# Modulation vector computed by VectorE with fused multiply-adds instead of by TensorE, twelve columns with two units each

## The chip, the cores and the metric

The kernel runs on one core of one Trainium2 chip. The metric is the device time of one execution in microseconds (us). Three runs before the change took 3199.53, 3201.83 and 3201.86 us; the median is 3201.83 us.

## The reference

The reference is one layer of a first block (a SwiGLU feed-forward, an attention and a state-space branch, a second SwiGLU feed-forward, an embedding gate, each with a layer norm) followed by one layer of a second block, all in float32. The change concerns two places of it:

```python
x = layer_norm(ALPHA * x + 0.5 * swiglu(x, ffn1_w1, ffn1_w3, ffn1_w2), ln1_g, ln1_b)   # first feed-forward
...
mod   = silu(c)     @ mod_w + mod_b     # second block: shift, scale, gate of the tokens
mod_k = silu(c_ctx) @ mod_w + mod_b     # and of the context
```

x has 1024 tokens by 1024 features; mod_w is 1024 by 3072, and c and c_ctx are one vector of 1024 numbers each. The modulation (the two vectors of 3072 numbers) depends on nothing else, and is first used by the context in the middle of the kernel. Both kernels compute it beside the first feed-forward.

## The kernel before

**Layout and engines.** Activations lie transposed, features on the 128 partitions and tokens along the free axis. Every float32 weight block is split by ScalarE into a rounded high part (type fp32r) and by VectorE into the rest, the low part, and a product takes three fp32r matmuls a block (high by high, high by low, low by high). Each engine's program is written out in a fixed order; engines wait for each other through semaphores, and each works strictly in its order.

**The columns of the feed-forward.** The hidden layer has 22 columns of 128 features, n = 0 to 21. From column 2 on a Strassen-like scheme computes the two up-projections of a column by seven products, m1 to m7, of 12 matmuls of 512 tokens each. Four weight sums (s1 to s4, done by `sums`, in four VectorE instructions) feed m5, m6, m7 and m3. VectorE adds the products up (`u2`, `c11`, `u3`, two in `c22`, `c21`, `c12`), ScalarE and VectorE make the hidden rows of both halves of the tokens (`mul`, then a high and a low part, `m_low` being the low one). The order is written out by `product_steps` (lines 31 to 52): for a column m2, m6, m5, m7, then, in even columns up to 18, a "down" step, then the modulation units of the column, then m1 of the next column, m4 and m3. The down step g adds the hidden columns 2g and 2g+1 into X: 16 groups of 6 matmuls, each read out of PSUM by one VectorE instruction. Down 0 stands inside column 2.

**Weights in flight.** A weight tile of 128 by 1024 float32 (512 KB) is loaded by SyncE into one of four raw slots (RAW has three, RAWX is the fourth). SyncE issues the loads in one fixed order and waits before each for the last reader of what lay in the slot (line 3564). Which slot a tile gets is settled by `lay_out` (line 145): the one whose present tile is read for the last time earliest in the order. The tile u1[n] (first up-projection, column n) serves m1 and m2 and, summed with u3[n], m5, m6, m7 and m3; u3[n] serves m4 too. The split halves lie in a ring of six places of 512 columns. In every step each engine calls `release` for the unit that it has finished, and `release` calls `halves`, which takes the next units in order, as far as their place and their raw slot are free in the order of the program, and splits them. So the split of a unit stands in the program about six units ahead of its product. `halves` of VectorE also does the sums of a column, one unit ahead of m6's own split (`sum_at`, line 379), and they wait until u3[n] has landed (line 2217).

**The modulation before.** A unit is a tile of mod_w, 256 input features by 512 outputs, 24 units in all (six output blocks m of four units). Each is split like any weight, and TensorE multiplies it by the split vectors silu(c), silu(c_ctx) (CVS, 4 columns) in 4 matmuls of 512 columns into PSUM bank 7, which is kept for it (the ring of banks has 7 others). After four units ScalarE copies the [4, 512] result to HELD, TensorE turns it in four small transposes (`mod_turn`), and VectorE adds up high and low and the bias into MOD. Columns 3, 5, 7 and 9 have two units, the others one.

Of the kernel before, what the change touches and what calls it, by code (L numbers as in the profile page):

```python
# [33 lines left out]
def product_steps(with_mod):  # L34


    out, mods = [], 0
    for n in range(2, 22):
        if 2 < n < 21:
            out.append(("m2", n))  # L40
        out.append(("m6", n))
        if n == 2:
            out.append(("down", 0))
        out += [("m5", n), ("m7", n)]
        if 2 < n < 19 and n % 2 == 0:
# [103 lines left out]
def lay_out(entries):  # L149
# [3 lines left out]
    for u, (kind, zone, loads, piece) in enumerate(entries):  # L153
        f = Form(kind, loads, piece)
        forms.append(f)
        if kind == "raw":
            continue
        if zone == "first" and base is None:
            base = [order[(at + i) % 5] for i in range(5)]
            ring, turn = [2 * k + i for k in base[:3] for i in range(2)], 0  # L160
        if zone == "ring":
            k = order[at % 5]
            at += 1
            f.places = (2 * k, 2 * k + 1)
# [41 lines left out]
    for u, f in enumerate(forms):  # L206
        f.raws = [ends[earlier[n]] for n in f.loads if n in earlier and forms[ends[earlier[n]]].kind == "raw"]
# [3 lines left out]
class Units:  # L211
# [10 lines left out]
    def next_half(self):  # L222

        while self.halved < self.limit:
            f = self.forms[self.halved]
            if not all(u in self.left for u in f.before + f.raws):
                return None
            self.halved += 1
            if f.kind not in ("raw", "hold"):
                return self.halved - 1  # L230
# [16 lines left out]
def build(nc, t, plan):  # L247
# [42 lines left out]
    CVS = at("CVS", 206, [128, 8, 4], F32R)  # L290
# [70 lines left out]
    CHI, CLO = CVS[:, :, 0:2], CVS[:, :, 2:4]  # L361
# [24 lines left out]
    banks, tmps, misc = Ring(7), Ring(NTMP), Ring(2)  # L386
# [144 lines left out]
    def tensor(e):  # L531
# [83 lines left out]
        def mod_turn(m):  # L615
            use = ("mt", m)
            banks.take(use, (ve, "mt", m))
            e.wait_ge(ac("mod", m), dma("const")("cols"), *banks.free(use))
            trs([(bank(*use)[:, 4 * j:4 * j + 4], HELD[0:4, m % 2, 128 * j:128 * j + 128], ident[0:4, 0:4])
                 for j in range(4)]).then_inc(*mm.inc(*use))  # L620

        def mod_unit(n):
            m, q = divmod(n, 4)
            if q == 0 and m:
                mod_turn(m - 1)
                e.wait_ge(ac("mod", m - 1))
            us = [w.take(), w.take()]
            e.wait_ge(w_hi(us[1]), w_lo(us[1]), ac("cvs"), ve("cvs"))
            mms([(PS[0:4, 7, :], CVS[:, 2 * q + k, :], blk(us[k], 0, 512)[r], q + k + r == 0, q + k + r == 5)
                 for k in range(2) for r in range(2)]).then_inc(*mm.inc("mod", n))  # L630
            for u in us:
                release(u)

        def ffn(name, tag, with_mod):
# [68 lines left out]
            for what, n in steps:  # L703
# [4 lines left out]
                elif what == "mod":  # L708
                    mod_unit(n)
# [7 lines left out]
            for m in range(4):  # L717
                down_open(m, last_parts(m))
                if m == 1 and with_mod:
                    mod_turn(5)  # L720
# [568 lines left out]
        banks.resize(8)  # L1289
        banks.ends[7] = ((ac, "mod", 5),)  # L1290
# [19 lines left out]
    def scalar(e):  # L1310
# [68 lines left out]
        def ffn(name, with_mod):  # L1379
# [38 lines left out]
            def mod_unit(n):  # L1418
                m, q = divmod(n, 4)
                us = [w.take(), w.take()]  # L1420
                if q == 3:
                    e.wait_ge(mm("mod", n))
                    if m > 1:
                        e.wait_ge(mm("mt", m - 2))
                    act(HELD[0:4, m % 2, :], PS[0:4, 7, :], ACT.Copy).then_inc(*ac.inc("mod", m))
                release(*us)

# [20 lines left out]
            for what, n in product_steps(with_mod):  # L1448
                if what == "mod":
                    mod_unit(n)  # L1450
                    continue
# [715 lines left out]
        act(CHI, cvec, ACT.Copy).then_inc(*ac.inc("cvs"))  # L2167
# [14 lines left out]
    def vector(e):  # L2182
# [112 lines left out]

        def mod_turn(m):
            e.wait_ge(mm("mt", m), dma("const")("cols"))
            part = bank("mt", m)[:, 0:16].rearrange("p (a r v) -> p a r v", a=4, r=2)
            out = MOD[:, 4 * m:4 * m + 4, :]
            tt(out, part[:, :, 0], col("mod_b", 4 * m, 4).unsqueeze(2).to_broadcast([128, 4, 2]), ALU.add).then_inc(*ve.inc("mt0", m))  # L2300
            e.wait_ge(ve("mt0", m))
            tt(out, out, part[:, :, 1], ALU.add).then_inc(*ve.inc("mt", m))

        def ffn(name, tag, with_mod, held):
# [99 lines left out]
            def mod_unit(n):  # L2404
                m, q = divmod(n, 4)
                if q == 0 and m:
                    mod_turn(m - 1)
                release(w.take(), w.take())

# [35 lines left out]
            for what, n in product_steps(with_mod):  # L2445
# [3 lines left out]
                if what == "mod":  # L2449
                    mod_unit(n)  # L2450
                    continue
# [43 lines left out]
            for m in range(8):  # L2495
                down_one(LAST, m, 0)
                if m == 1 and with_mod:
                    mod_turn(5)
# [1027 lines left out]
        e.wait_ge(ac("cvs"))  # L3526
        low(CLO, cvec, CHI).then_inc(*ve.inc("cvs"))
# [3 lines left out]
        ffn("ln1", "x", True, lambda h: mm("mt", 4 + h))  # L3531
# [23 lines left out]
    def sync(e):  # L3555
# [224 lines left out]
    for count in range(2):  # L3780
# [6 lines left out]
        banks.n = 7  # L3787
# [43 lines left out]
def ffn_units(w1, w3, w2, mod):  # L3831
# [17 lines left out]
    for what, n in product_steps(bool(mod)):  # L3849
# [15 lines left out]
        else:  # L3865
            if what == "down" and n == 0:
                forms.append(("hold", "hold", (), 0))
            for a in (down(columns_of(n)) if what == "down" else [mod[n]]):
# [148 lines left out]
```

## Time and profile before

| | us |
|---|---|
| median of three runs | 3201.83 |
| the profiled execution | 3202.06 |
| its span, first to last instruction | 3200.3 |
| TensorE busy (14840 matmuls) | 3126.6, 98% of the span |
| VectorE busy (4144 instructions) | 2400.2, 75% |
| ScalarE busy (1933 instructions) | 1240.3, 39% |

The profiled execution took 0.23 us more than the median of the runs, so its durations can be added to either. The chain that ended last is 88% TensorE, 7% VectorE and 4% ScalarE. Busy time of TensorE counts pipelined matmuls until their modelled end, so the distance from one start to the next, not the duration, says what a matmul costs in a stream.

### The profile page before, as it was taken

The numbers are of one execution on the slowest core, as the hardware profiler recorded it, in microseconds if no ns is written. First come the engines' busy times: TensorE is split into PE (matmuls) and PEld (weight loads), VectorE is DVE, ScalarE is ACT, GpSimd is POOL, SyncE is SP. The second block draws the span as 40 slices with busy tenths as digits, with TensorE's granted clock in tenths as the row PEclk, the third lists the DMA queues.
The fourth block names the chain that finished last, engine by engine and source line by source line (L and its number), as shares of the span: only waits on it lengthen the run. The fifth ranks groups of instructions, "written<-read, shape, count | busy, mean of one in ns | idle before, by whom it ended". The sixth has DMA issues, their size and how long they took to land.

```text
span 3200.3 us, 37931 instructions
## 1 busy us (share of the span) xinstructions
PE 3126.6 (98%) x14840; PEld 2543.1 (79%) x14840; DVE 2400.2 (75%) x4144; ACT 1240.3 (39%) x1933; POOL 2.2 (0%) x9
## 2 busy tenths in 40 slices
PE   8999999999999999988999999999999999999998
PEld 7887888877988877777887888888777688788887
DVE  6777777778869588878588766667788789789736
ACT  4333233335242456655243223223355533423414
POOL 0000000000000000000000000000000000000000
PEclk9999999999999999999999999999999999999999
DMA  3222211213433450002311111111211321122242
GB/s 128 73 79 77 68 66 66 73 60 126 130 82 130 142 190 8 7 27 74 151 53 47 60 46 53 60 47 53 66 53 53 112 70 70 40 77 97 78 168 73
DMA packets 89249, 250.68 MB, mean 78 GB/s; under 512 B 8560, under 2 KB 24304, under 8 KB 87536
## 3 DMA queue, kind: packets, MB, share of 16 engines
q1 hardware_dynamic: 89072, 248.25, 22.4%
q8 instruction: 119, 1.95, 0.2%
q14 instruction: 58, 0.48, 0.0%
HBM read 204.18 MB, written 44.04 MB: 78 GB/s over the span
## 4 chain that ended last, share of the span: by engine, by line
PE 88%; DVE 7%; ACT 4%; issue 1%; DMA 0%; DVEq 0%; SPq 0%; ACTq 0%
PE PS L543 86%; PE PS L548 2%; DVE WS L2187 1%; DVE X L2195 1%; DVE XS L2195 1%; DVE X L2187 1%; ACT PT L1314 1%; ACT TMP L1792 1%; DVE HELD L2244 1%; DVE COLB L2995 1%; ACT XS L1314 0%; DVE XSf L2187 0%; DVE TMP L2187 0%; DVE PT L2187 0%; ACT WS L1314 0%
## 5 line engine op out<-in xcount | busy, mean ns | idle before, releaser
L543 PE MATMUL PS<-XS,WS 128*128 128x512 f32 (+1 forms) x6480 | 1515.7, 391 | 18.8 <-DVE XS L2187 8.7
L543 PEld LDWEIGHTS PS<-XS,WS 128*128 128x128 f32 x6480 | 1208.8, 188 | 294.5 <-issue 28.2
L543 PE MATMUL PS<-HS,WS 128*128 128x512 f32 x2208 | 512.5, 391 | 3.1 <-DVE TMP L2187 2.7
L543 PEld LDWEIGHTS PS<-HS,WS 128*128 128x128 f32 x2208 | 415.2, 188 | 93.6 <-DVE TMP L2187 3.5
L2187 DVE TENSOR_TENSOR WS<-RAW,WS 128x512 fp32r<-128x512 f32 (+1 forms) x403 | 353.4, 885 | 178.5 <-ACT WS L1314 177.9
L1314 ACT ACTIVATE WS<-RAW 128x512 fp32r<-128x512 f32 (+1 forms) x403 | 312.8, 782 | 404.6 <-PE PS L543 350.2
L2187 DVE TENSOR_TENSOR X<-PS,X 128x512 f32<-128x512 f32 x272 | 184.3, 689 | 101.7 <-PE PS L543 101.6
L2187 DVE TENSOR_TENSOR TMP<-TMP,PS 128x512 f32<-128x512 f32 x304 | 203.8, 683 | 65.5 <-PE PS L543 59.3
L543 PE MATMUL PS<-T,WS 128*128 128x512 f32 x960 | 230.6, 389 | 0.0
L543 PEld LDWEIGHTS PS<-T,WS 128*128 128x128 f32 x960 | 180.2, 188 | 37.4
L1314 ACT ACTIVATE TMP<-PS 128x512 f32<-128x512 f32 x144 | 85.0, 595 | 303.2 <-PE PS L543 299.6
L2195 DVE SCALAR_TENSOR_TENSOR CV<-UU,COL,CV 128x1024 f32<-128x1024 f32 x120 | 154.1, 1284 | 3.4
L1314 ACT ACTIVATE HS<-TMP 128x512 fp32r<-128x512 f32 x88 | 55.6, 632 | 210.4 <-DVE TMP L2195 196.3
L543 PE MATMUL PS<-KH,QH 128*128 128x512 f32 x384 | 109.0, 422 | 2.3 <-DVE QH L2187 2.3
L543 PE MATMUL PS<-T1h_ln,WS 128*128 128x512 f32 x320 | 105.0, 389 | 0.0
L2187 DVE TENSOR_TENSOR PT<-PS,PT 128x512 fp32r<-128x512 f32 x128 | 82.2, 683 | 15.5 <-ACT PT L1314 15.2
L1314 ACT ACTIVATE PT<-PS 128x512 fp32r<-128x512 f32 x128 | 69.8, 595 | 56.8 <-PE PS L548 55.6
L1314 ACT ACTIVATE TMP<-TMP 128x512 f32<-128x512 f32 x80 | 50.6, 632 | 101.4 <-DVE TMP L2187 101.4
L2187 DVE TENSOR_TENSOR HS<-TMP,HS 128x512 fp32r<-128x512 f32 x88 | 60.7, 689 | 32.3 <-ACT HS L1314 32.1
L1314 ACT ACT_TABLE_LOAD x56 | 71.8, 1283 | 32.8 <-DVE GG L2187 27.1
L543 PEld LDWEIGHTS PS<-KH,QH 128*128 128x128 f32 x384 | 70.4, 196 | 14.5 <-ACT VH L1314 2.5
L543 PE MATMUL PS<-MH,WS 128*128 128x512 f32 x256 | 80.4, 393 | 0.0
(334 smaller groups left out, 3628.7 us busy)
## 6 DMA issues: line engine op xcount, KB each, us to landing
RAW<-in_W SPq DMA_DIRECT2D x263, 512.0 KB, 3.3
RAWX<-in_W SPq DMA_DIRECT2D x30, 512.0 KB, 3.2
DC<-TMP SPq DMA_DIRECT2D x32, 256.0 KB, 2.0
X<-in_xT SPq DMA_DIRECT2D x8, 512.0 KB, 9.3
DX<-X SPq DMA_DIRECT2D x2, 2048.0 KB, 9.0
DCZ<-CA SPq DMA_DIRECT2D x8, 512.0 KB, 4.3
DGA<-TMP SPq DMA_DIRECT2D x16, 256.0 KB, 2.2
DGB<-TMP SPq DMA_DIRECT2D x16, 256.0 KB, 3.3
```

Source lines behind the costliest of these rows:

```text
L543: done = d.matmul(out, l, r, start=first, stop=last)
L548: done = d.transpose(out, x, idn)
L1314: return d.activation(out, x, f, bias=bias, scale=scale)
L1792: d.activation(PROB[n % 3], PS[:, 2 + 2 * (n % 2):4 + 2 * (n % 2), :], ACT.Exp, bias=nb, scale=SCALE, accum_out=sm).then_inc(*ac.inc("ex", n))
L2187: return d.tensor_tensor(out, a, b, op)
L2195: return d.scalar_tensor_tensor(out=out, in0=a, scalar=s, in1=b, op0=op0, op1=op1)
L2244: d.reciprocal(out[:, 0:width], tmp("rs", name, h)[:, 0:width]).then_inc(*ve.inc("rs", name, h))
L2995: d.tensor_reduce(mx, PS[:, 2 + 2 * (n % 2):4 + 2 * (n % 2), :], AX.XY, ALU.max).then_inc(*ve.inc("mx", n))
```

## The change

The 24 units keep their tiles and their order, but are no longer split. For each unit VectorE runs four instructions on [128, 512]: for each of its two row blocks and each of the two vectors it multiplies the raw tile by the vector's column of 128 numbers (a scalar per partition) and adds to HELD. After four units TensorE sums HELD over the partitions: 8 float32 matmuls (4 blocks of 128 outputs by 2 vectors) with HELD as the weights and one column of ones as the moving operand, which leaves the outputs on the partitions; VectorE adds the bias. In the order two units stand in columns 2, 3, 5, 6, 8, 9, 11, 12, 14, 15, 17 and 18, and a turn at the end of columns 4, 7, 10, 13, 16 and 19. The units get a kind of their own, "vec": no place in the ring of six, and a raw slot that is free once VectorE's fourth instruction is done. The sums of a column move from the unit before m6 to m6 itself, in both feed-forwards. Bank 7 joins the ring of PSUM banks (8 instead of 7).

```diff
@@ product_steps
-        if with_mod:
-            for _ in range(2 if n in (3, 5, 7, 9) else 1):
-                out.append(("mod", mods))
-                mods += 1
+        if with_mod and n < 20 and n % 3 != 1:
+            out += [("mod", mods), ("mod", mods + 1)]
+            mods += 2
         out += [("m1", n + 1) if n < 21 else ("m2", n), ("m4", n), ("m3", n)]
+        if with_mod and n % 3 == 1 and n < 20:
+            out.append(("turn", mods // 4 - 1))
@@ lay_out
-        if kind == "raw":
+        if kind in ("raw", "vec"):
             continue
...
-        f.raws = [... forms[ends[earlier[n]]].kind == "raw"]
+        f.raws = [... forms[ends[earlier[n]]].kind in ("raw", "vec")]
@@ build
-            sum_at[u if pieces[0] == u - 2 else min(u, pieces[1])] = f.loads
+            sum_at[u] = f.loads
-    banks, tmps, misc = Ring(7), Ring(NTMP), Ring(2)
+    banks, tmps, misc = Ring(8), Ring(NTMP), Ring(2)
@@ tensor
         def mod_turn(m):
             use = ("mt", m)
             banks.take(use, (ve, "mt", m))
-            e.wait_ge(ac("mod", m), dma("const")("cols"), *banks.free(use))
-            trs([(bank(*use)[:, 4 * j:4 * j + 4], HELD[0:4, m % 2, 128 * j:128 * j + 128], ident[0:4, 0:4])
-                 for j in range(4)]).then_inc(*mm.inc(*use))
-        def mod_unit(n):
-            ... (waits for both halves, 4 matmuls into PS[0:4, 7, :])
+            e.wait_ge(ve("mv", 4 * m + 3), ve("ones"), *banks.free(use))
+            for j in range(4):
+                for v in range(2):
+                    done = d.matmul(bank(*use)[:, 2 * j + v:2 * j + v + 1], HELD[:, v, 128 * j:128 * j + 128], ones[:, 0:1],
+                                    start=True, stop=True)
+            done.then_inc(*mm.inc(*use))
@@ scalar
-        def mod_unit(n):
-            ... (copies PS[0:4, 7, :] to HELD after every fourth unit)
@@ vector
+        def mod_unit(n):
+            m, q = divmod(n, 4)
+            u = w.take()
+            e.wait_ge(*loaded(u), ac("cv"))
+            for k in range(2):
+                for v in range(2):
+                    x, c = HELD[:, v, :], cvec[:, 2 * q + k, v:v + 1]
+                    if q + k == 0:
+                        d.tensor_scalar(x, raw(u, 512 * k, 512), c, None, ALU.mult).then_inc(*ve.inc("ms", n, k, v))
+                    else:
+                        e.wait_ge(ve("ms", n, 0, v) if k else ve("ms", n - 1, 1, v))
+                        stt(x, raw(u, 512 * k, 512), c, x, ALU.mult, ALU.add).then_inc(*ve.inc("ms", n, k, v))
+            ve.same("mv", n)
+            ve.same("vec", u)
+            release(u)
@@ sync, loads
-                    e.wait_ge(mm("unit", u) if forms[u].kind == "raw" else w_lo(u))
+                    e.wait_ge(mm("unit", u) if forms[u].kind == "raw" else ve("vec", u) if forms[u].kind == "vec" else w_lo(u))
@@ ffn_units
+            if what == "mod":
+                forms.append(("vec", "turning", (load(mod[n]),), 0))
```

The rest of the diff takes out what the old way needed: the tile CVS and its two instructions, the turn of the last block after the products, and the steps that kept bank 7.

## Rows read from the trace of the kernel before

**Rows 1.** The page, busy time, share and instructions of each engine.

```profile
PE 3126.6 (98%) x14840; PEld 2543.1 (79%) x14840; DVE 2400.2 (75%) x4144; ACT 1240.3 (39%) x1933; POOL 2.2 (0%) x9
```

**Rows 2.** Busy time in the stretch of the columns; TensorE, loads, VectorE, ScalarE, POOL, clock, DMA.

```profile
90.00:655.00 565.00, 564.32 (x2498) 456.11 (x2497) 402.96 (x635) 184.81 (x312) 0.00 (x0) 1.00 0.21 72
```

**Rows 3.** The chain of waits, 60 to 700 us: start, length, what (one piece).

```profile
240.92 0.59 ACT HELD L1314
```

**Rows 4.** TensorE in order of time: start, duration, what.

```profile
114.02 2.02 PE L543 MATMUL PS<-WS,CVS 128*4 128x512 f32 x8
115.88 2.92 PE L543 MATMUL PS<-XS,WS 128*128 128x512 f32 x12
...
176.79 0.41 PE L548 MATMUL PS<-ident,HELD 4*128 4x4 f32 x4
177.12 2.01 PE L543 MATMUL PS<-WS,CVS 128*4 128x512 f32 x8
...
366.74 1.09 PE L543 MATMUL PS<-WS,CVS 128*4 128x512 f32 x4
367.67 2.92 PE L543 MATMUL PS<-XS,WS 128*128 128x512 f32 x12
370.42 2.88 PE L543 MATMUL PS<-T,WS 128*128 128x512 f32 x12
```

**Rows 5.** Weight loads in order of time: start, duration, what.

```profile
1015.47 1.98 PEld L543 LDWEIGHTS PS<-KM,UB 128*128 128x128 f32 x16
1017.36 1.68 PEld L543 LDWEIGHTS PS<-XS,WS 128*128 128x128 f32 x8
```

**Rows 6.** Groups of weight loads by shape: busy, mean ns, idle before.

```profile
L543 PEld LDWEIGHTS PS<-HELD,ones 128*128 128x128 f32 x26 | 4.5, 188 | 7.9 <-DVE HELD L2187 6.8 <-issue 0.5
L543 PEld LDWEIGHTS PS<-WS,CVS 128*4 128x4 f32 x96 | 7.7, 85 | 10.9 <-issue 0.3
```

**Rows 7.** VectorE in order of time: start, duration, what, idle before.

```profile
366.94 0.69 DVE L2187 TENSOR_TENSOR TMP<-TMP,PS 128x512 f32<-128x512 f32 x1 [1.36 <-PE PS L543]
367.54 0.68 DVE L2187 TENSOR_TENSOR RAW<-RAW,RAWX 128x512 f32<-128x512 f32 x1
...
370.07 0.69 DVE L2187 TENSOR_TENSOR WS<-RAW,WS 128x512 fp32r<-128x512 f32 x1
...
374.46 0.69 DVE L2195 SCALAR_TENSOR_TENSOR TMP<-TMP 128x512 f32<-128x512 f32 x1
376.37 0.69 DVE L2187 TENSOR_TENSOR WS<-RAW,WS 128x512 fp32r<-128x512 f32 x1 [1.22 <-ACT WS L1314]
...
379.49 0.68 DVE L2195 SCALAR_TENSOR_TENSOR TMP<-TMP 128x512 f32<-128x512 f32 x1
380.88 0.69 DVE L2187 TENSOR_TENSOR HS<-TMP,HS 128x512 fp32r<-128x512 f32 x1 [0.70 <-ACT HS L1314]
...
707.46 0.74 DVE L2195 SCALAR_TENSOR_TENSOR XS<-X,COL,XS 128x512 fp32r<-128x512 f32 x1
708.12 0.74 DVE L2195 SCALAR_TENSOR_TENSOR X<-X,COL,HELD 128x512 f32<-128x512 f32 x1
```

**Rows 8.** A VectorE group by shape: busy, mean ns, idle before.

```profile
L2191 DVE TENSOR_SCALAR TMP<-ident,COLB 128x128 f32<-128x128 f32 x64 | 18.4, 287 | 2.3
```

**Rows 9.** DMA issues, 300 to 500 us: KB each, us from issue to landing.

```profile
RAW<-in_W SPq DMA_DIRECT2D x20, 512.0 KB, 3.3
```

**Rows 10.** Half a microsecond each behind the issue at 399.21 us; last columns DMA share, GB/s.

```profile
400.20:400.70 0.50, 0.50 (x4) 0.42 (x3) 0.16 (x1) 0.00 (x0) 0.00 (x0) 1.00 0.92 311
...
401.20:401.70 0.50, 0.50 (x3) 0.39 (x3) 0.03 (x1) 0.00 (x0) 0.00 (x0) 1.00 0.82 328
```

**Rows 11.** Two microseconds each around TensorE's idle stretch; the clock is third from the end.

```profile
64.00:66.00 2.00, 0.48 (x3) 0.05 (x1) 1.97 (x4) 0.51 (x1) 0.00 (x0) 1.00 0.74 258
66.00:68.00 2.00, 1.51 (x5) 1.25 (x6) 2.00 (x4) 0.33 (x1) 0.00 (x0) 0.84 0.75 227
68.00:70.00 2.00, 2.00 (x6) 1.55 (x5) 2.00 (x5) 2.00 (x4) 0.00 (x0) 0.50 0.84 236
70.00:72.00 2.00, 2.00 (x8) 1.60 (x8) 2.00 (x5) 2.00 (x5) 0.00 (x0) 0.80 0.16 66
```

More of the change, by code:

```diff
@@ L206, in lay_out @@
     for u, f in enumerate(forms):
-        f.raws = [ends[earlier[n]] for n in f.loads if n in earlier and forms[ends[earlier[n]]].kind == "raw"]
+        f.raws = [ends[earlier[n]] for n in f.loads if n in earlier and forms[ends[earlier[n]]].kind in ("raw", "vec")]
     return forms, slots, earlier, ends
@@ L228, in next_half @@
             self.halved += 1
-            if f.kind not in ("raw", "hold"):
+            if f.kind not in ("raw", "vec", "hold"):
                 return self.halved - 1
@@ L289, in build @@
     HELD = at("HELD", 202, [128, 2, 512], F32)
-    CVS = at("CVS", 206, [128, 8, 4], F32R)
     HS = at("HS", 152, [128, NHS, 2, 1024], F32R)
@@ L360, in build @@
     ACf = at("ACf", 152, [128, 2, 4, 1024], F32)
-    CHI, CLO = CVS[:, :, 0:2], CVS[:, :, 2:4]
     cvec, STAT, GL = COLB[:, 0:16].rearrange("p (k v) -> p k v", v=2), COLB[:, 32:64], COLB[:, 64:96]
@@ L617, in mod_turn @@
             banks.take(use, (ve, "mt", m))
-            e.wait_ge(ac("mod", m), dma("const")("cols"), *banks.free(use))
-            trs([(bank(*use)[:, 4 * j:4 * j + 4], HELD[0:4, m % 2, 128 * j:128 * j + 128], ident[0:4, 0:4])
-                 for j in range(4)]).then_inc(*mm.inc(*use))
-        def mod_unit(n):
[L623 to L632, printed above, removed]
+            e.wait_ge(ve("mv", 4 * m + 3), ve("ones"), *banks.free(use))
[4 more added lines that the diff above has]
+            done.then_inc(*mm.inc(*use))
         def ffn(name, tag, with_mod):
@@ L708, in ffn @@
                 elif what == "mod":
-                    mod_unit(n)
+                    release(w.take())
+                elif what == "turn":
+                    mod_turn(n)
                 else:
@@ L718, in ffn @@
                 down_open(m, last_parts(m))
-                if m == 1 and with_mod:
-                    mod_turn(5)
             for m in range(8):
@@ L1288, in tensor @@
         ffn("ln1", "x", True)
-        banks.resize(8)
-        banks.ends[7] = ((ac, "mod", 5),)
         latents()
@@ L1416, in turned @@
                     act(hi(k), lo(k), ACT.Copy).then_inc(*ac.inc(name, what, k))
-            def mod_unit(n):
[L1419 to L1426, printed above, removed]
             us = {fi: (w.take(), w.take()) for fi in (0, 1)}
@@ L1448, in ffn @@
             for what, n in product_steps(with_mod):
+                if what == "turn":
+                    continue
                 if what == "mod":
-                    mod_unit(n)
+                    release(w.take())
                     continue
@@ L2166, in scalar @@
         e.wait_ge(ac("cv"))
-        act(CHI, cvec, ACT.Copy).then_inc(*ac.inc("cvs"))
         ffn("ln1", True)
@@ L2294, in norm @@
                     yield
+        def mod_unit(n):
[13 more added lines that the diff above has]
+            release(u)
         def mod_turn(m):
             e.wait_ge(mm("mt", m), dma("const")("cols"))
-            part = bank("mt", m)[:, 0:16].rearrange("p (a r v) -> p a r v", a=4, r=2)
             out = MOD[:, 4 * m:4 * m + 4, :]
-            tt(out, part[:, :, 0], col("mod_b", 4 * m, 4).unsqueeze(2).to_broadcast([128, 4, 2]), ALU.add).then_inc(*ve.inc("mt0", m))
-            e.wait_ge(ve("mt0", m))
-            tt(out, out, part[:, :, 1], ALU.add).then_inc(*ve.inc("mt", m))
+            tt(out, bank("mt", m)[:, 0:8].rearrange("p (a v) -> p a v", v=2),
+               col("mod_b", 4 * m, 4).unsqueeze(2).to_broadcast([128, 4, 2]), ALU.add).then_inc(*ve.inc("mt", m))
         def ffn(name, tag, with_mod, held):
@@ L2402, in turned @@
                 low(lo, f, hi).then_inc(*ve.inc(name, what, k))
[L2404 to L2408, printed above, removed]
             def down_one(g, m, h):
@@ L2450, in ffn @@
                     mod_unit(n)
+                    continue
+                if what == "turn":
+                    mod_turn(n)
                     continue
@@ L2496, in ffn @@
                 down_one(LAST, m, 0)
-                if m == 1 and with_mod:
-                    mod_turn(5)
                 norm_add(name, m, 0, X, x_now, held(0))
@@ L3525, in vector @@
         halves()
-        e.wait_ge(ac("cvs"))
-        low(CLO, cvec, CHI).then_inc(*ve.inc("cvs"))
         e.wait_ge(dma("const")("cols"))
@@ L3530, in vector @@
         tt(DB, col("ln2_b", 4, 4), col("ln2_b", 0, 4), ALU.subtract).then_inc(*ve.inc("db"))
-        ffn("ln1", "x", True, lambda h: mm("mt", 4 + h))
+        ffn("ln1", "x", True, lambda h: mm("mt", 5))
         latents()
@@ L3786, in build @@
             ring.restart()
-        banks.n = 7
+        banks.n = 8
     for s in signals.values():
@@ L3867, in ffn_units @@
                 forms.append(("hold", "hold", (), 0))
-            for a in (down(columns_of(n)) if what == "down" else [mod[n]]):
+            for a in down(columns_of(n)) if what == "down" else ():
                 k = load(a)
                 forms += [("cols", "turning", (k,), 0), ("cols", "turning", (k,), 1)]
+            if what == "mod":
+                forms.append(("vec", "turning", (load(mod[n]),), 0))
     for j, a in enumerate(down(columns_of(LAST))):
```

## The prediction

> **What bounds the kernel now.** I read the page first: TensorE is busy 98% of the span, VectorE 75% [rows 1]. Then the stretch of the changed columns, 90 to 655 us: TensorE idles 0.7 us in 565, VectorE works 403 us, 71% [rows 2]. So a matmul taken out shortens the kernel by its whole spacing, and one put in lengthens it; VectorE's work is free as long as its results come before TensorE asks for them. Next TensorE in order of time, for spacings: a product of 12 matmuls takes 2.72 to 2.75 us from start to start (367.67 to 370.42) [rows 4], 0.227 us a matmul, so a down group of 6 takes 1.36. Last VectorE in order of time and the loads, because the change makes both late.
>
> **TensorE's part.** Removed: a single unit holds 0.93 us (366.74 to 367.67), a pair 1.86 (114.02 to 115.88), a turn of four transposes 0.33 (176.79 to 177.12) [rows 4]. 16 singles 14.9, 4 pairs 7.4, 6 turns 2.0; ScalarE's copy to HELD stood in the chain once, 0.6 [rows 3]. Sum 24.9 us. Added: 48 float32 matmuls. The trace counts a float32 matmul twice (the layer norms' sums of ones by HELD have two records each, 26 for 13 [rows 6]), so a turn is 16 weight loads with 16 matmuls of one column. The nearest rows are 16 loads of the same shape in 1.89 us (1015.47 to 1017.36), 0.118 each, beside matmuls of 128 columns [rows 5]. I take 2.1 us a turn with its start, 12.5 in all. Bounds: the spacing of the old turn's transposes, 0.083 us [rows 4], 8 us in all; the whole length of a load, 0.188 [rows 6], 18 us. Net on TensorE: 12.4 us less.
> A load of 128 columns is 103 ns longer than one of 4, 0.83 ns a column [rows 6]. The Trainium skill (TensorE: Matmul & The Clock Gate, LDWEIGHTS) gives the columns over 1.2 GHz, by itself 107 ns for 128; the turns would be 10.2 us by it instead of 12.5.
>
> **VectorE's part.** Removed: 48 low halves at 0.60 us from start to start. Added: 96 instructions with a column of scalars; the like ones run 0.66 apart (707.46 to 708.12) [rows 7]. That is 63 less 29 us, 34 more: 437 of some 550 us, 80%. On average it fits. I price all 96 alike: the 12 with one tensor operand could be faster, but a TENSOR_SCALAR of 128 elements takes 287 ns [rows 8].
> By the Trainium skill (VectorE: DVE Perf Modes, Mode 2x_2P) a float32 operation with a single tensor source in SBUF makes two elements a cycle; those 12 would save VectorE 3 us, which changes the kernel by less than 1. The 84 with two tensors stay at one, which is what speaks against the change.
>
> **The new wait.** Before, a unit's raw slot came free with its split, about six units ahead of its use. Now it comes free only when VectorE has done the unit in its place. By the rule of the layout (the slot whose tile is read last earliest), in all twelve columns the first unit of the pair has the slot that u3[n+1] needs. So VectorE finishes the first unit and calls `release`; the next thing in its program is the sums of column n+1, which need u3[n+1], whose load SyncE issues only now. VectorE stands for the whole load, 3.3 us [rows 9]; its second unit, the splits and the product sums of the next steps are queued behind it, and ScalarE stands in its own program at the high part of that sum. From the landing, four sums take 2.53 us and the low half of m6 0.69 (367.54 to 370.07) [rows 7]. TensorE needs m6 of column n+1 four products, 10.9 us, after the modulation step. I write the time since TensorE began m1 (t = 0).
>
> *Odd column after an unloaded one (5, 11, 17).* VectorE takes up m7 at 0.2 (366.94 against 366.74), adds `u3` and both `c22`, starts the unit at 2.0, has it done at 4.7; load to 8.1; low half of m6 done at 11.3. TensorE waits 0.4. Then the other low half, the second unit, and the column's steps with the waits for ScalarE that rows show: 1.91 us from `mul` to the low half behind it, 1.39 from `mul` to the next `m_low` [rows 7]. The hidden rows of the column are done at 20.5 and 23.8. TensorE wants them for the down step at 19.5: it waits 1.0, runs one group, waits 1.9. In the down column itself u1[n+2] lies in the slot of the second down tile, whose last split is the unit just before it; VectorE stands for another load and its high half, the last `c22` ends at 33.5, and the seventh down group, which needs that PSUM bank among the eight, wants it at 30.6: 2.9. Together 6.2 us, three times: 18.6.
> *Even column (6, 8, 12, 14, 18).* The last group is read at once, the unit starts at 0.9, m6 is ready at 10.2, before 10.9. No wait there.
> *Odd column right after a loaded one (9, 15; 3 is like it).* VectorE is already late: second unit of column 8 done at 13.4, low half of m7 at 14.0. Only then are issued, in one order, the loads of two modulation tiles and of u1[n+1]. A transfer holds the DMA engines some 1.4 us (400.2 to 401.7) [rows 10], so the third lands at 19.6; its high and low half are ready at 21.0, TensorE wants m1 at 19.0: 2.0. The rest of the column takes VectorE 9.5 us (ten starts at 0.60 to 0.70 and two waits of 0.7 to 0.8), so the next first unit starts at 29.8, is done at 32.5, its load lands at 35.9, m6 is ready at 39.1, wanted at 31.9: 7.2. The hidden rows are ready at 48.3 and 51.6, wanted from 47.3: 1.0 and 1.9. Together 12.1 us; columns 9 and 15: 24.2. At columns 2 and 3, where m5 and m7 stand between down 0 and the first unit, the same working gives 13.3.
> *Columns 7 to 8 and 13 to 14*: the turn gives VectorE 2.1 us; 0.4 us remain each, 0.8.
> Waits in all: 57 us. Bounds: nothing, if VectorE's lead covers all of it; and 12 waits of 3.3, 8 later waits of 3.9 for u1 and the 34 us of work, all uncovered, 105.
>
> **The clock.** After an idle stretch of 2 us before 66.5 TensorE's clock was granted at 0.84, 0.50 and 0.80 in three stretches of 2 us: 1.7 us lost at the lower level, 1.2 GHz [rows 11]. The three waits of 7 us should bring it down each time. Most of the loss only uses up the wait that follows (VectorE, not TensorE, sets the next step); I add 4 us, bounds 0 and 20 (twelve waits of 1.7).
>
> **Hidden edits.** Taking 48 high halves from ScalarE, the sums one unit later and CVS are worth nothing: ScalarE works 185 us of 565 [rows 2] and the sums stand five products ahead; uncovered, the sums' move costs 0.6 us a column. The eighth bank is in the working above; with seven, the down waits would be 1.4 us longer.
>
> **Sum.** 3202.1 (the profiled execution, 0.2 above the median of the runs) - 12.4 + 57 + 4 = 3250.7; I say 3250.
>
> **Rivals.**
> A, faster: VectorE's lead hides everything. For it: 29% of VectorE is idle now [rows 2], a split has five products, 13.6 us, before its use, and a down step gives VectorE slack for 12 us. Against it: m6's split has four products and a load in it. Then only TensorE's net counts: 3202 - 12 = 3190. It decides if VectorE starts the first unit within some 1.5 us of TensorE's m1 and never falls more than 10.9 us behind in the odd columns.
> B, about even: the units cost their work, but the loads are not waited for, because the slots fall otherwise than I read them, or a load lands by the time VectorE comes to it. VectorE is then 5.3 us late per pair instead of 9 to 13; only the odd columns after loaded ones reach TensorE, three times 2 to 6 us and some clock: 3202 - 12 + 16 = 3206.
> C, slower still: VectorE sets the pace for most of the stretch, since each wait leaves the next step later than my chains carry over and the loads queue. VectorE's work 437, its waits for ScalarE now 60 or so, 12 loads of 3.3 and 8 of 3.9, and the part of its idle time in down steps that can't be used, some 50: 617 us for a stretch of 565 before, 3202 + 52; with the clock at 1.2 GHz after most waits, 20, and turns at 18 us, 3280 to 3290.
>
> **Chances.** Forecast 0.58, A 0.10, B 0.13, C 0.19. For the likeliest alone 3225 to 3275. The range leaves out A and half of C: 3203 to 3285. A change under 0.2% (6.4 us) can't be told from none. B lies on that line and is split between same and slower: faster 0.10, same 0.07, slower 0.83.
>
> **What would show it.** In the profile after: the 96 and 24 matmul records of the old way gone and 96 of the turns there, a turn near 2 us. VectorE waiting for the DMA of RAW, a dozen times near 3.3 us, right behind its fourth instruction on HELD. TensorE waiting for WS (m6, m1) and for HS (down) in the stretch from 90 us, some 57 us in all, the longest near 7 us in columns 3, 9 and 15, and clock below 1.00 behind them; the second feed-forward unchanged. If VectorE never waits for RAW, the slot step is wrong (B); if it does and TensorE doesn't wait, my count of the lead is wrong (A); if the gain on TensorE isn't near 12 us, the turns are.

## The result, and the profile after

The change made the kernel slower: 3241.02 us, the median of 4 runs (3239.27 to 3242.18), against 3201.28 in the same session (3199.53 to 3201.86). The ratio is 1.0123, 95% interval 1.0112 to 1.0135. The forecast was 3250 and slower. The execution profiled after has a span of 3240.4 us, 40.1 more than before.

The page of the changed kernel answers to [rows 1]: TensorE does 2 points less of a longer span, with nearly the same busy time. The second block is the stretch of the columns, answering to [rows 2] (busy of TensorE, weight loads, VectorE, ScalarE, POOL, then clock, DMA share, GB/s): 43 us of 605 without a matmul where it was 0.7 of 565, and a clock of 0.98.

```profile
PE 3123.4 (96%) x14816; PEld 2548.2 (79%) x14816; DVE 2419.9 (75%) x4185; ACT 1205.0 (37%) x1878; POOL 2.2 (0%) x9
```
```profile
90.00:695.00 605.00, 561.71 (x2471) 459.71 (x2470) 424.74 (x679) 151.26 (x260) 0.00 (x0) 0.98 0.19 68
```

Next the view of waits in 80 to 690 us: who waits for what, us in total, times, the longest. TensorE first.

```profile
PE PS L542 <- ACT WS L1302: 23.5, 5, 6.9
PE PS L542 <- DVE HS L2166: 9.5, 9, 1.7
PE PS L542 <- DVE TMP L2166: 7.6, 5, 2.4
PE PS L542 <- DVE WS L2166: 2.7, 1, 2.7
```

VectorE in the same stretch. Before, there was no wait of VectorE for a tile of weights here. Now there are twelve of 3.3 us. The releaser reads "issue" because the profile ties none to them; the times of the load below do.

```profile
DVE WS L2166 <- ACT WS L1302: 84.5, 49, 5.1
DVE RAW L2166 <- issue: 36.4, 11, 3.4
...
DVE RAWX L2166 <- issue: 3.4, 1, 3.4
```

One of them in order of time (start, duration, engine, what, count, idle before). The pair of column 8 begins at 295.80. Its first unit is done at 298.0; at 298.03 SyncE issues the next load of its queue (it issued none between 274.3 and then); the sums, which need that tile, start at 301.34. After the second unit (305.08, done at 307.8) VectorE stands again, now because ScalarE's high half of m1 is not made.

```profile
295.80 0.87 DVE L2283 TENSOR_SCALAR HELD<-RAW,COLB 128x512 f32<-128x512 f32 x2
296.59 1.41 DVE L2174 SCALAR_TENSOR_TENSOR HELD<-RAW,COLB,HELD 128x512 f32<-128x512 f32 x2
301.34 0.69 DVE L2166 TENSOR_TENSOR RAW<-RAW 128x512 f32<-128x512 f32 x1 [3.34 <-issue]
...
305.08 2.73 DVE L2174 SCALAR_TENSOR_TENSOR HELD<-RAWX,COLB,HELD 128x512 f32<-128x512 f32 x4
...
314.93 0.69 DVE L2166 TENSOR_TENSOR WS<-RAW,WS 128x512 fp32r<-128x512 f32 x1 [5.11 <-ACT WS L1302]
```

That second stop is the load of u1: SyncE's rows show three loads going out together when the second unit is done, and u1 is the last.

```profile
307.84 0.33 SPq L3553 DMA_DIRECT2D RAWX<-in_W  x1
308.21 0.91 SPq L3553 DMA_DIRECT2D RAW<-in_W  x2
```

TensorE in order of time, the first 350 us (the later columns repeat these waits within 0.2 us; the last row is cut off where the view ends). In turn: m1 and m6 of column 3, its hidden row; a turn and the two products behind it; the three waits of columns 5 and 6, two for hidden rows and one for a PSUM bank; a bank; m1, m6 and a hidden row of column 9.

```profile
113.11 2.98 PE L542 MATMUL PS<-XS,WS 128*128 128x512 f32 x12 [2.69 <-DVE WS L2166]
131.02 5.19 PE L542 MATMUL PS<-T,WS 128*128 128x512 f32 x12 [6.77 <-ACT WS L1302]
143.36 20.65 PE L542 MATMUL PS<-HS,WS 128*128 128x512 f32 x90 [0.33 <-DVE HS L2166]
172.01 1.84 PE L620 MATMUL PS<-ones,HELD 128*128 128x1 f32 x16
173.71 3.03 PE L542 MATMUL PS<-XS,WS 128*128 128x512 f32 x12
176.57 2.88 PE L542 MATMUL PS<-T,WS 128*128 128x512 f32 x12
204.65 1.61 PE L542 MATMUL PS<-HS,WS 128*128 128x512 f32 x6 [0.68 <-DVE HS L2166]
207.94 7.05 PE L542 MATMUL PS<-HS,WS 128*128 128x512 f32 x30 [1.68 <-DVE HS L2166]
217.29 15.49 PE L542 MATMUL PS<-HS,WS 128*128 128x512 f32 x60 [2.31 <-DVE TMP L2166]
281.22 13.94 PE L542 MATMUL PS<-HS,WS 128*128 128x512 f32 x60 [0.35 <-DVE TMP L2166]
315.72 3.01 PE L542 MATMUL PS<-XS,WS 128*128 128x512 f32 x12 [1.53 <-ACT WS L1302]
333.76 4.57 PE L542 MATMUL PS<-T,WS 128*128 128x512 f32 x12 [6.87 <-ACT WS L1302]
346.29 3.88 PE L542 MATMUL PS<-HS,WS 128*128 128x512 f32 x16 [1.15 <-DVE HS L2166]
```

Last the clock around the wait before 333.76, in windows of 2 us, answering to [rows 11]; it is the third figure from the end. TensorE works 0.24 us of the first window and all of the two others; the clock is 0.50, 0.50, then 0.71.

```profile
332.00:334.00 2.00, 0.24 (x1) 0.27 (x2) 2.00 (x4) 1.79 (x4) 0.00 (x0) 0.50 0.01 4
334.00:336.00 2.00, 2.00 (x5) 1.57 (x6) 2.00 (x4) 0.36 (x1) 0.00 (x0) 0.50 0.03 8
336.00:338.00 2.00, 2.00 (x8) 1.62 (x7) 2.00 (x4) 0.00 (x0) 0.00 (x0) 0.71 0.12 18
```

Below, "the clock's loss" of a run is worked out in one way for all: stretches of 4 us from 80 to 690 us, in each TensorE's busy time times what the granted clock lacks to 1.00, summed. It is 0.0 us before and 7.0 after.

### The profile page after: what moved, and what is told of

It is laid out like the page before. It is cut to its first block, busy times and chain, and to the rows that moved or that the text cites. A ratio compares the mean times of both kernels' runs of the same rounds, so it can differ in the third digit from the quotient of the medians.

```text
span 3240.4 us, 37839 instructions
## 1 busy us (share of the span) xinstructions
PE 3123.4 (96%) x14816; PEld 2548.2 (79%) x14816; DVE 2419.9 (75%) x4185; ACT 1205.0 (37%) x1878; POOL 2.2 (0%) x9
## 4 chain that ended last, share of the span: by engine, by line
PE 69%; DVE 7%; ACT 4%; issue 1%; DMA 0%; DVEq 0%; ACTq 0%; SPq 0%
PE PS L542 67%; PE PS L547 2%; DVE WS L2166 1%; DVE X L2174 1%; DVE XS L2174 1%; DVE X L2166 1%; ACT PT L1302 1%; DVE COLB L2983 1%; ACT TMP L1772 1%; DVE HELD L2223 1%; ACT XS L1302 0%; DVE TMP L2166 0%; DVE XSf L2166 0%; DVE PT L2166 0%; ACT WS L1302 0%
## 5 line engine op out<-in xcount | busy, mean ns | idle before, releaser
L2166 DVE TENSOR_TENSOR WS<-RAW,WS 128x512 fp32r<-128x512 f32 (+1 forms) x373 | 333.2, 900 | 208.1 <-ACT WS L1302 207.9
L1302 ACT ACTIVATE WS<-RAW 128x512 fp32r<-128x512 f32 (+1 forms) x373 | 292.9, 795 | 352.0 <-PE PS L542 270.6
L542 PE MATMUL PS<-T,WS 128*128 128x512 f32 x960 | 236.5, 396 | 20.6 <-ACT WS L1302 20.6
L2166 DVE TENSOR_TENSOR TMP<-TMP,PS 128x512 f32<-128x512 f32 x304 | 202.7, 682 | 54.2 <-PE PS L542 47.9
L542 PEld LDWEIGHTS PS<-T,WS 128*128 128x128 f32 x960 | 183.9, 192 | 60.6 <-ACT WS L1302 21.7
L1302 ACT ACTIVATE WS<-S2T 128x512 fp32r<-128x512 f32 x40 | 25.3, 633 | 278.8 <-DVE S2T L2166 256.8
```

Of the source, the lines that this page charges most:

```text
L542: done = d.matmul(out, l, r, start=first, stop=last)
L1302: return d.activation(out, x, f, bias=bias, scale=scale)
L2166: return d.tensor_tensor(out, a, b, op)
```

## The experiments

The theory of places: a unit's tile keeps its place until VectorE has worked on it, the next column's tiles must wait for that place, and their loads are what TensorE ends up waiting for. The rival, the theory of work: the 96 instructions, 60 us of VectorE (84 start 0.66 apart, 12 start 0.40 apart; the expectations below say 64) in place of 29 us of low halves, use up its lead whatever the loads do. Edits are made to the changed kernel unless another is named. The runs of the kernel before beside the first four had a median of 3201.6.

**One: the first unit is given up with the second.** Since VectorE takes splits in the order in which units are given up, it now does both units and then the sums.

```
-            release(u)
+            if n % 2:
+                release(u - 1, u)
```

> VectorE frees the raw slots and splits the next units only after the second unit of a pair; instructions, loads and their order are the same. Slot theory (VectorE stands for the load of u3[n+1] behind the first unit, and everything behind it comes late): the second unit's 2.65 us now lie under the load, so VectorE's twelve waits of 3.35 us shrink to about 0.7. All that comes behind the second unit is 2.65 us earlier: at columns 5/6, 11/12 and 17/18 TensorE's waits for the hidden rows (0.7 and 1.7 us) and for the PSUM bank (2.3) go to nothing; at 9, 15 and 3 the wait before m1 (1.5) goes, the one before m6 falls from 6.9 to about 4.2, the one for the hidden rows goes. Waits 43 to about 13 us, with some clock: 3205 us (3200 to 3212). Work theory (it is VectorE's 34 us more of work that TensorE waits for, the load wait only stands where VectorE would have been idle): the same work in the same place, 3230 us or more.

3209.49 us (3206.22 to 3212.28), ratio to before 1.0023 [1.0012, 1.0033]. The load goes out at 289.11, VectorE does its second unit meanwhile, and the sums wait 0.95 us instead of 3.34:

```profile
287.67 1.41 DVE L2174 SCALAR_TENSOR_TENSOR HELD<-RAW,COLB,HELD 128x512 f32<-128x512 f32 x2
288.99 2.73 DVE L2174 SCALAR_TENSOR_TENSOR HELD<-RAWX,COLB,HELD 128x512 f32<-128x512 f32 x4
292.68 0.69 DVE L2166 TENSOR_TENSOR RAW<-RAW 128x512 f32<-128x512 f32 x1 [0.95 <-issue]
```

The same instructions in another order give back 32 of the 40 us. Between the two profiled executions, 30.5 us apart, 25.1 lie before the end of the block; the other 5.4 lie behind it, where the programs are the same, and are not the edit's. TensorE's waits fall from 43.3 to 18.5 us, while the clock's loss is 9.8 in the execution that was profiled (3211.69 us, on the long side of this kernel's).

**Two: no tile, the same work.** The 24 loads and their places are gone; VectorE's 96 instructions read rows of X instead. The modulation is then of the wrong data.

```
-                forms.append(("vec", "turning", (load(mod[n]),), 0))
+                forms.append(("vec", "turning", (), 0))
...
-                        d.tensor_scalar(x, raw(u, 512 * k, 512), c, None, ALU.mult)
+                        d.tensor_scalar(x, X[:, 2 * q + k, 0:512], c, None, ALU.mult)
...
-                        stt(x, raw(u, 512 * k, 512), c, x, ALU.mult, ALU.add)
+                        stt(x, X[:, 2 * q + k, 0:512], c, x, ALU.mult, ALU.add)
```

> The 24 units have no tile and no raw slot; VectorE runs the same 96 instructions in the same places, on rows of X instead (the modulation is not what it should be: this leaves out the 24 loads). Slot theory: no wait for a load, u3 and u1 are in their slots early, TensorE's waits in the columns go to under 3 us; what is left is the gain of TensorE (14 us on the columns, 3 us on the first down step, 2 us given back behind the first feed-forward): 3187 us (3183 to 3193). Work theory: the work is unchanged, so at least half of the waits stay: 3215 us or more.

3184.11 us (3183.29 to 3186.41), ratio 0.9946 [0.9931, 0.9961]. TensorE waits 1.2 us in 60 to 700, the clock loses nothing. This is the theory of work tried alone, and it falls: all of that work fits beside TensorE. It also gives the change's worth without its places, 17.5 us faster, and the price of the places, 3241.0 - 3184.1 = 56.9 us.

**Three: half the work, all the places.** Only the first row block of each unit is added up, so half of the modulation's sum is left out.

```
-            for k in range(2):
+            for k in range(1):
...
-                        e.wait_ge(ve("ms", n, 0, v) if k else ve("ms", n - 1, 1, v))
+                        e.wait_ge(ve("ms", n - 1, 0, v))
```

> Each unit runs only the two instructions of its first row block (half of the modulation's sum is left out); tiles, slots, loads and the order stay. VectorE's work on the units is then 32 us, about the 29 of the low halves that it replaced. Slot theory: VectorE still waits 3.35 us for u3[n+1] in the twelve columns; the columns are earlier by 1.3 us a unit, which leaves waits of about 3 us before m6 at columns 4, 10 and 16 and little else, some 9 us with a little clock: 3197 us (3192 to 3204), not down to the 3187 of no load wait. Work theory: with no work added nothing is left of the waits: 3187 us. If the two effects only add up, without one needing the other, the waits fall by the share of the work removed, about 34 of 74 us: 3217.

3220.76 us (3219.24 to 3227.24), ratio 1.0058 [1.0041, 1.0074]: a miss, 24 us above what I expected from my own theory, and near the 3217 that I had written down for two effects that only add up. I had let the waits shrink by the work taken out. The trace (of the execution of 3227.24 us, 6.5 above the median) shows VectorE's waits whole: VectorE stands 44 us for tiles, more than the 39.8 of the full version (one of them 4.67 us), and TensorE's waits for m6 go only from 6.9 to 5.7.

```profile
DVE RAW L2166 <- issue: 40.1, 11, 4.7
DVE RAWX L2166 <- issue: 3.9, 1, 3.9
```

**Four: seven banks until the end of the block.** (The line that sets the ring to seven where the program starts anew is left out below.)

```
-    banks, tmps, misc = Ring(8), Ring(NTMP), Ring(2)
+    banks, tmps, misc = Ring(7), Ring(NTMP), Ring(2)
...
         ffn("ln1", "x", True)
+        banks.resize(8)
```

> Seven PSUM banks in the ring through the first feed-forward, as before the change, eight behind it; all else as after. If the eighth bank is what took 3 us off the first down step (its second group waited 2.0 us before and the clock fell behind it), this comes back; and the waits for a bank in the down steps of columns 6, 12 and 18 (2.3 us), 8 and 14 (0.3) each grow by the length of one group, 1.4. In all some 10 us more than the changed kernel: 3251 us (3246 to 3256). If the down step's gain is from elsewhere (the fewer splits of ScalarE): 3248 or less, with the first down step unchanged.

3261.73 us (3259.89 to 3267.28), ratio 1.0190 [1.0175, 1.0205]: 20.7 more than the change, twice what I expected and above my range. Its parts in the block, by the traces: 2.7 us in the first down step (below); TensorE's waits in 80 to 690 us 54.2 instead of 43.3, so 10.9, most of it in the bank waits (4.20 where eight banks have 2.31, 4.53 where they have 2.28); and the clock, which loses 14.0 instead of 7.0. Together 20.6. The two profiled spans are only 17.7 apart, since behind the block this one is 4.3 shorter. I had left the clock out. The first down step, seven banks and then eight (the kernel before has 2.01 us there too):

```profile
66.22 22.29 PE L542 MATMUL PS<-HS,WS 128*128 128x512 f32 x90 [2.01 <-DVE TMP L2167]
88.35 0.39 PE L542 MATMUL PS<-T1h_ln,WS 128*128 128x512 f32 x1
```
```profile
66.41 19.36 PE L542 MATMUL PS<-HS,WS 128*128 128x512 f32 x84 [0.63 <-DVE TMP L2166]
85.61 0.39 PE L542 MATMUL PS<-T1h_ln,WS 128*128 128x512 f32 x1
```

**Five: all the places, less work still.** To settle the third run's miss, the 84 multiply-adds are cut to 16 of 512 columns, so that most of the modulation's sum is left out. It does not take all the work away: 84 at 0.15 us and 12 multiplications at 0.40 are 17 us, where half the work was 29 and the whole is 60.

```
-                        stt(x, raw(u, 512 * k, 512), c, x, ALU.mult, ALU.add)
+                        x = x[:, 0:16]
+                        stt(x, raw(u, 512 * k, 16), c, x, ALU.mult, ALU.add)
```

> The changed kernel with its 24 loads, their places and their order, but the 84 multiply-adds of the units work on 16 of 512 columns (12 full multiplications stay), so that nearly all of VectorE's 64 us of added work is gone; the modulation's values are therefore not the reference's. Halving the work before left 3221. If time is a sum of a part for places and one that falls in step with the work: 3221 - (3241 - 3221) = 3201 (range 3197 to 3206). If the load's landing sets the waits and the work between hardly counts any more: 3208 to 3221.

3218.28 us (3216.45 to 3219.75), ratio 1.0049 [1.0034, 1.0064]. The additive guess falls, though by less than the expectation has it, which took all the work for gone: 31 us of work less gave 20.3 us in the third run, so 12 less would give 8 here, and 2.5 came. The other outcome, 3208 to 3221, holds. The pair of column 8 shows why so little is left to gain. The two units' instructions take 1.7 us instead of 4.8, and VectorE stands 4.13 us for u3 and then 5.06 for the high half of m1, whose tile was the last of three loads that went out from 294.40 to 295.35, and was read by ScalarE at 300.77:

```profile
285.46 0.38 DVE L2174 SCALAR_TENSOR_TENSOR HELD<-RAW,COLB,HELD 128x16 f32<-128x16 f32 x2
289.96 0.69 DVE L2166 TENSOR_TENSOR RAW<-RAW 128x512 f32<-128x512 f32 x1 [4.13 <-DMA RAW<-in_W]
...
293.70 0.67 DVE L2174 SCALAR_TENSOR_TENSOR HELD<-RAWX,COLB,HELD 128x16 f32<-128x16 f32 x4
...
301.44 0.69 DVE L2166 TENSOR_TENSOR WS<-RAW,WS 128x512 fp32r<-128x512 f32 x1 [5.06 <-ACT WS L1302]
```

So some 34 of the 56.9 us (3218.3 - 3184.1) stay with 17 of the 60 us of work. By the rows of this pair they are two landings in a row, with VectorE's and ScalarE's programs held behind them; with no work at all it wasn't tried. The other 23 go with 43 us of work, which costs only because the landings have used up the lead (the second run has the whole work at no cost).

**Six and seven: another placement.** One unit in every column, and a second one in four odd columns only. By the layout's rule the next column's two tiles should then take places of earlier splits, except behind the four pairs. In the seventh run the pairs are deferred as in the first.

```
+        turn = with_mod and mods // 4
-        if with_mod and n < 20 and n % 3 != 1:
-            out += [("mod", mods), ("mod", mods + 1)]
-            mods += 2
+        if with_mod:
+            for _ in range(2 if n in (3, 5, 9, 11) else 1):
+                out.append(("mod", mods))
+                mods += 1
...
-        if with_mod and n % 3 == 1 and n < 20:
+        if with_mod and mods // 4 > turn:
```

> One modulation unit in every column 2 to 21, a second one in columns 3, 5, 9 and 11 (always an odd column, and never the end of one group of four and the start of the next in one column); each sum over the partitions stays behind the last unit of its four. The work of VectorE and TensorE is that of the change to the instruction; what differs is that after a single unit the next column's two weight tiles no longer take a place that a unit of the same column must leave first. Theory of places (the waits are loads that find their place held by a unit): only the four pairs are left, each worth what a loaded odd column followed by an even one cost there, some 5 to 7 us with the clock, so 3184 + 4 x 6 = 3208, range 3196 to 3214. Theory of work (64 us more of VectorE in these columns use up its lead): no better than the change, 3235 to 3245.

3204.44 us (3202.11 to 3206.68), ratio 1.0008 [0.9999, 1.0018]. VectorE stands for a tile four times, 13.9 us in all, instead of twelve times and 39.8.

```
-            release(u)
+            if n not in (1, 4, 9, 12):
+                release(*((u - 1, u) if n in (2, 5, 10, 13) else (u,)))
```

> The placement of the kernel just named, and in the four columns with two units the first one is given up (for the order in which VectorE takes its splits) only together with the second, so that VectorE does both before it waits for the tile that goes to the first one's place. Theory of places: each pair costs 3 us less, 3196, range 3188 to 3204, and so faster than the kernel before or equal to it. If what is left in the kernel just named is not VectorE's wait for that tile, the two are equal within 3 us.

3192.43 us (3191.76 to 3193.47), ratio 0.9970 [0.9958, 0.9981]: faster than the kernel before. VectorE's work is that of the change; deferring four pairs is worth 12.0 us, the 3 each that were expected. Waits of TensorE in the seventh run, 80 to 690 us, all of them:

```profile
PE PS L544 <- DVE HS L2168: 3.2, 1, 3.2
PE PS L544 <- ACT WS L1304: 1.6, 3, 1.1
```

**Eight: done by column 19, as in the change.** Six deferred pairs (columns 3, 5, 9, 11, 15, 17), nothing in columns 20 and 21; edits to the seventh run's kernel.

```
-        if with_mod:
-            for _ in range(2 if n in (3, 5, 9, 11) else 1):
+        if with_mod and n < 20:
+            for _ in range(2 if n in (3, 5, 9, 11, 15, 17) else 1):
...
-            if n not in (1, 4, 9, 12):
-                release(*((u - 1, u) if n in (2, 5, 10, 13) else (u,)))
+            if n not in (1, 4, 9, 12, 17, 20):
+                release(*((u - 1, u) if n in (2, 5, 10, 13, 18, 21) else (u,)))
```

> Two units in columns 3, 5, 9, 11, 15 and 17, one in the other columns 2 to 19, none behind column 19; in each pair the first unit is given up with the second. Against the version with one unit in columns 20 and 21 too (3192.4) it takes away the one long wait left there, 3.2 us of TensorE in front of the last tiles, whose place was a unit's, and adds two pairs, each worth about 0.5 us by the pairs already there (1.6 us of waits for conversions on four). Theory of places: 3192.4 - 3.2 - a little clock + 1 = 3190, range 3186 to 3193. Were a pair dear in itself, 3195 or more.

3188.14 us (3186.9 to 3189.52), ratio 0.9957 [0.9945, 0.9970]. This is the version that beats both kernels: 14 us under the one before, 53 under the change, 4 above the version without tiles. It has all 24 loads and all the work, so neither the traffic of the loads nor the work is what cost 57 us. Its TensorE waits 2.3 us in 60 to 690, and its clock loses nothing.

**Nine: the banks behind the block.** In all versions with eight banks from the start TensorE waits 3.7 us at a place of the attention where it didn't before. The eighth run has:

```profile
1171.42 4.50 PE L544 MATMUL PS<-CKV,WS 128*128 128x512 f32 x12 [3.68 <-DVE TMP L2168]
1186.06 2.99 PE L544 MATMUL PS<-KH,QH 128*128 128x512 f32 x12 [0.30 <-DVE QH L2168]
1188.89 2.21 PE L544 MATMUL PS<-CQ,WS 128*128 128x512 f32 x9
```

The edit to the eighth run's kernel moves the ring on by five, so that later uses get their old banks.

```
         ffn("ln1", "x", True)
+        for _ in range(5):
+            banks.skip()
```

> The kernel just named, and behind the first feed-forward block the ring of eight PSUM banks is moved on by five places, so that the latents and the attention behind take the banks that they took before the change (316 uses modulo 7 is place 1; modulo 8 it is 4). In every version with eight banks from the start TensorE waits 3.7 us for one bank in the attention, and in none where the later stages kept the old banks. If that wait is the banks' phase: 3.5 us less than the kernel just named, range 2 to 5 less. If it is only put off (the stretch behind has other waits of VectorE that then grow), 0 to 1.5 us less: the changed kernel lost 2.1 us behind the block in all.

3194.59 us (3191.7 to 3196.58), ratio to before 0.9977 [0.9967, 0.9986]: 6.4 us slower than without it (4.7 between the profiled spans), a miss. The shift lands on the most recently used banks, which VectorE is still adding to X, and TensorE waits 6.86 us at once:

```profile
705.02 10.05 PE L544 MATMUL PS<-XS,WS 128*128 128x512 f32 x36 [6.86 <-DVE X L2170]
```

The wait of 3.68 us is gone, so it is indeed the banks' phase. But it was hardly worth anything: TensorE now waits 2.33 us for QH a little later (as it does in the kernel before) and has the 12 matmuls behind it in 4.57 instead of 2.99 us, and it waits 0.4 us at each of two places between. The ninth run is 5.03 us behind the eighth in front of this stretch (1139.76 against 1134.73, a row of matmuls on ZG) and 4.46 us at its end (1193.35 against 1188.89), so 0.6 us came back. The wait was put off, the other outcome that the expectation names.

```profile
1188.94 4.57 PE L544 MATMUL PS<-KH,QH 128*128 128x512 f32 x12 [2.33 <-DVE QH L2170]
1193.35 2.21 PE L544 MATMUL PS<-CQ,WS 128*128 128x512 f32 x9
```

A shift at a quieter place wasn't tried; by these rows it could win some 0.6 us.

## Why the prediction was right, and where its sizes were off

The sign, the mechanism and the place hold: a load is issued only when VectorE has done the first unit, twelve times, 3.3 us each as [rows 9] has it; the runs on order, places and work make it the cause (all 56.9 us go with the places, and 53 of them with another order of the same loads and instructions). By the steps:

- **TensorE's part**: forecast 12.4 us less, measured 13.9 less. That is the 24.9 removed, as read from the rows before, less the turns. A turn runs from 172.01 to 173.71, and the product behind it takes 2.86 us to the next start (176.57) instead of 2.72, so a turn costs 1.84; six are 11.0 against 12.5. The second run, whose TensorE waits for nothing in these columns, bears the sum out: it reaches the end of the block 17.4 us before the kernel before (700.77 against 718.16, the same row), of which 3.0 are the first down step. The weight loads of a turn start 0.112 us apart (172.12 to 173.57 in thirteen steps). The Trainium skill (TensorE: Matmul & The Clock Gate, LDWEIGHTS) gave 107 ns for 128 columns, and the trace agrees within 5 ns; the turns by it, 10.2 us, were the better price than 12.5.
- **The waits**: forecast 57. The trace shows 43.3 of idle time; a matmul's modelled end lies 0.16 us behind the start of a following one (167.70 + 1.75 against 169.29), so each of the 20 waits is that much longer, 46.5 in all. By kind, forecast (the 13.3 of columns 2 and 3, which the prediction gives only in all, divided like the others) and idle shown: m6 after a loaded column 21.7 and 20.6; m1 6.7 and 5.7; banks 9.5 and 7.6; the small waits for m6 1.6 and 0. The step that was mis-sized is the hidden rows, 17.4 and 9.5. At columns 5, 11 and 17 it held (2.9 forecast, 2.27 to 2.41 shown). At 3, 9 and 15 I put the same 2.9 behind the 7 us wait, and there only 0.3 to 1.2 are seen. The likely reason, argued and not tried: behind those waits TensorE ran at the lower clock and came to the down step some 2 us later.
- **The clock**: forecast 4, measured 7.0. The three long waits lose 1.7 to 2.3 us each, where the prediction let most of the loss vanish in the wait that follows, and the first bank wait 1.4 (15.49 instead of 13.94 us for 60 matmuls). The last two errors offset in part: 10 too much of waits, 3 too little of clock.
- **The eighth bank**: I counted it only behind the modulation. It also serves the first down step, which ends 3.0 us earlier (88.63 to 85.61 us; run four takes 2.7 of it back). The prediction had this at nothing.
- **Behind the block**: forecast nothing, measured +2.1 us net (the row at 718.16 before stands at 756.17 after, 38.0 later, and the spans are 40.1 apart). The 3.7 us bank wait of the ninth run is hardly in it: 37.7 us at 1093 (of the kernel before) have become 38.4 at 1223, behind it. Another 1.6 come between 1516 and 2391; why is open. Nor is it the change's alone: from the block to the end the profiled executions of runs one to eight, with the same program there but for the banks, take from 3.3 us less to 1.9 us more than the kernel before.
- **Sum**: -13.9 - 3.0 + 46.5 + 7.0 + 2.1 = 38.7 of the 40.1 between the spans.
- **VectorE's prices**: the 84 instructions with two tensors start 0.66 apart, as read from [rows 7]. The 12 TENSOR_SCALARs start 0.40 apart (295.80, two of them, next row at 296.59). I priced them at 0.66 from [rows 8]; the Trainium skill (VectorE: DVE Perf Modes, Mode 2x_2P) had two elements a cycle for them, and the trace agrees. It is 3 us of VectorE's time; no run shows what they were worth to the kernel.
- **The rivals**: A's premise, that VectorE's lead covers the work, is true as soon as no load stands in it (3184 there, 3190 forecast), and false with the loads. B's mechanism was tried in parts: the first run removes most of the wait for u3 and not that for u1, and gives 3209 for B's 3206. B also charged the work 16 us without load waits; run two shows nothing. C had each wait leave the next step later than the chains carry over; the waits came out below the chains' 57 us, and the second run has the whole work with 1.2 us of waits.

## What to carry to other kernels

When work moves from the engine that bounds to one with idle time, count where its input tile lies and until when, before counting its busy time. Here 60 us of instructions in place of 29 were free as long as no load stood before them, and 24 tiles held a little longer cost 57 us, because the next column's loads queue for the places and come out one behind the other. The cure was order, not less work: spread the units so that the next needed tile seldom takes a place that is given up last, and where two stand together finish both before waiting. A ring of banks that continues always hands out the oldest one; shifting it to repair a later collision hands out the newest.

## What the runs showed of the hardware that was not expected

- Less idle time did not mean less loss of clock. TensorE's waits and the clock's loss in the same 610 us were 43.3 and 7.0 after the change, 27.2 and 9.6 with half the work, 20.8 and 8.7 with 17 us of it, 18.5 and 9.8 with deferred pairs. The longest waits were 6.9, 5.7, 4.8 and 4.7 us. Each is one execution, and the loss differs from one to the next: of the kernel with deferred pairs 3211.69 us was profiled, at a mean granted clock of 0.993, while others of it took 3206.3 at 0.995; with half the work it was the longest of four.
- A wait of about 2 us is no fixed price: 60 matmuls behind one of 1.90 us took 15.50 us and behind one of 1.88 us 13.94, both in the first run; in the fifth it was 13.89 behind 2.33 and 15.50 behind 2.49.
- Three loads of 512 KB issued within 1 us (the row of two above starts its second at 308.21 + 0.91 - 0.33 = 308.79): the last was read by ScalarE 5.4 to 5.5 us after its own issue and 6.4 after the first, where one alone takes 3.3. The same single load, of column 8, cost VectorE a wait of 3.34, 4.13 and 4.67 us in three runs (the change, the fifth and the third), at the same place of the program; why is open.
- An instruction on 128x16 elements with two tensors costs VectorE some 0.15 us (0.67 for four), against 0.66 for 512 columns.
